# The last feed-forward's down blocks as seven products of halves, with two sums' low parts on GpSimd a block later

## What is computed

```python
def swiglu(h, w_gate, w_up, w_down):
    return (jax.nn.silu(h @ w_gate) * (h @ w_up)) @ w_down

h = modulate(rms_norm(x, g_ffn[l]), sh_f, sc_f)
x = x + gt_f[:, None, :] * swiglu(h, w_gate[l], w_up[l], w_down[l])
```

## The kernel before

| part | gate, up | down |
|---|---|---|
| A, nt 8 | 19 to 26 | 27 to 30 |
| B, nt 8 | 31 to 38 | 39 to 42 |
| C, nt 6 | 43 to 48 | 49 to 52 |

## Time and profile before

### The profile page before, as it was taken

The page is one execution under the profiler, slowest core; times in us unless marked ns, Lnnn a source line. Parts: engine busy times, 40 slices in busy tenths (PEclk is TensorE's granted clock), DMA queues, the critical chain, the costliest instruction groups (busy, mean ns, idle before and its releaser), DMA issues.

```text
span 2032.4 us, 29841 instructions
## 1 busy us (share of the span) xinstructions
PE 2026.5 (100%) x10896; PEld 1712.4 (84%) x10896; DVE 1220.5 (60%) x2142; ACT 894.1 (44%) x1361; POOL 1038.9 (51%) x773
## 2 busy tenths in 40 slices
PE   9999999999999999999999999999999999999999
PEld 7788778889889878877788899898877788989898
DVE  5677335576757637854356767567445478647363
ACT  4124353536446422244445355364446544536352
POOL 5454334476555754443355755556343334656555
PEclk9999999999999999999999999999999999999999
DMA  6332212343543343321233443433221212233233
GB/s 223 107 104 84 83 63 101 117 166 105 187 147 124 104 130 101 104 83 64 82 111 128 142 151 144 166 104 104 97 85 66 80 42 104 84 104 105 104 104 104
DMA packets 37492, 223.99 MB, mean 110 GB/s; under 512 B 6012, under 2 KB 6524, under 8 KB 11744
## 3 DMA queue, kind: packets, MB, share of 16 engines
q1 hardware_dynamic: 31424, 193.48, 27.7%
q10 hardware_dynamic: 5920, 28.55, 4.1%
HBM read 215.59 MB, written 2.10 MB: 107 GB/s over the span
## 4 chain that ended last, share of the span: by engine, by line
PE 98%; DVE 1%; DVEq 0%; issue 0%; ACT 0%; ACTq 0%
PE ps L599 18%; PE ps L601 18%; PE ps L600 18%; PE ps L756 6%; PE ps L758 6%; PE ps L757 6%; PE ps L616 4%; PE ps L617 4%; PE ps L618 4%; PE ps L684 2%; PE ps L648 1%; PE ps L650 1%; PE ps L649 1%; PE ps L705 1%; PE ps L694 1%; PE ps L726 0%
## 5 line engine op out<-in xcount | busy, mean ns | idle before, releaser
L519 POOL TENSOR_TENSOR w_lo<-w_raw,w_hi 128x512 fp32r<-128x512 f32 x544 | 732.0, 1377 | 775.8 <-ACT w_hi L1168 766.5
L1168 ACT ACTIVATE w_hi<-w_raw 128x2048 fp32r<-128x2048 f32 x134 | 256.1, 1911 | 383.5 <-PE ps L601 290.7
L599 PE MATMUL ps<-a_hi,w_hi 128*128 128x512 f32 (+1 forms) x888 | 352.2, 397 | 0.0
L601 PE MATMUL ps<-a_hi,w_lo 128*128 128x512 f32 (+1 forms) x888 | 346.2, 390 | 0.0
L600 PE MATMUL ps<-a_lo,w_hi 128*128 128x512 f32 (+1 forms) x888 | 345.8, 389 | 0.0
L533 POOL TENSOR_TENSOR w_lo<-w_raw,w_hi 128x512 fp32r<-128x512 f32 x164 | 214.6, 1331 | 160.9 <-ACT w_hi L1295 160.9
L599 PE MATMUL ps<-b_hi,w_hi 128*128 128x512 f32 x612 | 238.1, 389 | 0.0
L600 PE MATMUL ps<-b_lo,w_hi 128*128 128x512 f32 x612 | 238.1, 389 | 0.0
L601 PE MATMUL ps<-b_hi,w_lo 128*128 128x512 f32 x612 | 238.1, 389 | 0.0
L599 PEld LDWEIGHTS ps<-a_hi,w_hi 128*128 128x128 f32 (+1 forms) x888 | 165.3, 186 | 48.0 <-issue 9.7
L601 PEld LDWEIGHTS ps<-a_hi,w_lo 128*128 128x128 f32 (+1 forms) x888 | 165.3, 186 | 36.8
(11 more groups left out here) (394 smaller groups left out, 4523.6 us busy)
## 6 DMA issues: line engine op xcount, KB each, us to landing
w_raw<-in_weights SPq DMA_DIRECT2D x176, 1024.0 KB, 4.9
v<-in_ada ACTq DMA_DIRECT2D x24, 1024.0 KB, 4.9
out<-x SPq DMA_DIRECT2D x8, 256.0 KB, 2.5
x<-in_x_in SPq DMA_DIRECT2D x3, 512.0 KB, 6.8
w_raw<-in_weights SPq DMA_DIRECT2D x4, 256.0 KB, 5.5
yc<-in_c_rows ACTq DMA_DIRECT2D x2, 512.0 KB, 3.2
bias<-in_mult_bias ACTq DMA_DIRECT2D x1, 640.0 KB
x<-in_x_in SPq DMA_DIRECT2D x2, 256.0 KB, 4.7
```

Source lines behind the costliest of these rows:

```text
L519: nc.gpsimd.tensor_tensor(w_lo[:, s, piece], w_raw[:, s, piece], f32(w_hi[:, s, piece]), ALU.subtract).then_inc(w_lo_ready, 1)
L599: nc.tensor.matmul(o, wh, hi(kt), start=kt == 0, stop=False)
L601: last = nc.tensor.matmul(o, wl, hi(kt), start=False, stop=kt == depth - 1)
L1168: nc.scalar.activation(w_hi[:, n % 2, :], w_raw[:, n % 2, :], ACT.Copy).then_inc(w_hi_ready, 1)
```

## The change

Eight of the twelve down blocks become fast blocks: 28, 29, 30, 40, 41, 42, 50 and 51. For these, seven products need token sums of h, four for each part. VectorE makes the raw sums (`h_forms`) as the tiles of h come, in every up block's turn. ScalarE rounds three of them ahead of its work on the first fast down block and the fourth, whose place is a quarter of h itself (in part C of `a_hi`), after the first down block. VectorE makes the low parts of the first two, ahead of `sum_low` (2) and of the x adds; GpSimd makes those of the other two ahead of the low parts of the second fast down block. The x add takes the fast block's results from `sums`.

To give the sums room, the scratch for DMA descriptors shrinks from 16 KB to 1 KB per partition, and t4's raw values share a place with other data. h's tiles and the down weights' rows are stored in the order of halves (`h_slot`). The gate block carries its columns twice, 64 apart: the second copy is replaced by its low part in place, so that 16 matmuls of 100 columns give both products, and VectorE adds the two groups of rows.

```diff
-FAST = [j for j, kind, *_ in feed_forward() if kind != "down" and j >= C_FF + 5]
+def fast_kind(j, kind, hid, b, nt):
+    if kind == "down":
+        return 0 < b - nt < (3 if nt == FF_TILES[-1] else 4)
+    return j >= C_FF + 5
+FIRST_DOWNS = [j for j, kind, hid, b, nt in feed_forward() if b == nt]
+FAST = [plan[0] for plan in feed_forward() if fast_kind(*plan)]
...
 GpSimd
+            def split_gates(n, s):
+                pool.wait_ge(w_hi_ready, n - 1)
+                raw, hi = (m[:, s, :].rearrange("p (k c) -> p k c", k=KT)[:, :, LOW_ROW:IF_ROWS] for m in (w_raw, w_hi))
+                nc.gpsimd.tensor_tensor(hi, raw, f32(hi), ALU.subtract).then_inc(w_lo_ready, 4)
+            def h_sum_low(part_, i):
+                hi, lo = (m[:, 0:FF_TILES[part_] // 2, :] for m in h_sums[part_][i])
+                pool.wait_ge(ht_hi, 4 * part_ + T_ORDER.index(i) + 1)
+                nc.gpsimd.tensor_tensor(lo, h_sums_f32[i][:, 0:FF_TILES[part_] // 2, :], f32(hi), ALU.subtract
+                                        ).then_inc(ht_late, 1)
...
+                if n - LAYERS * LAYER_BLOCKS - 2 in FIRST_DOWNS:
+                    for i in T_ORDER[2:4]:
+                        h_sum_low(FIRST_DOWNS.index(n - LAYERS * LAYER_BLOCKS - 2), i)
                 if n in FAST_BLOCKS:
                     split_fast(n, FAST_BLOCKS.index(n))
...
 PE
+            def gate_rows(t, s):
+                pe.wait_ge(bank_free[t % 4], nth(L, LAYER_BANKS, BANK_USES[t]))
+                pe.wait_ge(w_lo_ready, nth(L, 4 * LAYER_BLOCKS, 4 * C_IF + 3))
+                for kt in range(KT):
+                    for part in (a_hi, a_lo):
+                        last = nc.tensor.matmul(ps[t % 4][0:IF_ROWS, :], wcols(w_hi, s, KT, kt, 0, IF_ROWS), part[:, kt, :],
+                                                start=kt == 0 and part is a_hi, stop=kt == KT - 1 and part is a_lo)
+                last.then_inc(tile_done, 2)
...
+                    if j in FAST:
+                        fast_block(L, FF, FAST.index(j), j, FAST_USES[j], (b_hi, b_lo), h_sums[part_], nt // 2,
+                                   lambda i: pe.wait_ge(ht_split if i < 2 else ht_late, 2 * part_ + T_ORDER.index(i) % 2 + 1))
...
 ScalarE, next_weights(j) with f = j + 1
                 column_high(f, 0).then_inc(w_hi_ready, 1)
+                if j in FIRST_DOWNS:
+                    for i in T_ORDER[0:3]:
+                        h_sum_high(FIRST_DOWNS.index(j), i)
                 if j in FAST:
                     p1_copy_out(L, FF, FAST.index(j))
...
+            def h_sum_high(part_, i):
+                act.wait_ge(ht_raw, 4 * part_ + T_ORDER.index(i) + 1)
+                deep = FF_TILES[part_] // 2
+                nc.scalar.activation(h_sums[part_][i][0][:, 0:deep, :], h_sums_f32[i][:, 0:deep, :], ACT.Copy).then_inc(ht_hi, 1)
...
 ScalarE, end of evict(j, u)
+                if j in FIRST_DOWNS and u == 1:
+                    h_sum_high(FIRST_DOWNS.index(j), T_ORDER[3])
...
 VectorE
+                def h_forms(n):
+                    far, i = divmod(n, nt // 2)
+                    t1, t2, t3, t4 = (m[:, i, :] for m in h_sums_f32)
+                    left, right = g[:, 6 + n % 2, 0:HS], g[:, 6 + n % 2, HS:S]
+                    if far == 0:
+                        tt(t1, left, right, ALU.subtract)
+                        nc.vector.tensor_copy(t3, right)
+                        return
+                    nc.vector.scalar_tensor_tensor(t2, right, -1.0, t1, ALU.mult, ALU.subtract)
+                    tt(t3, right, t3, ALU.subtract)
+                    dve.drain()
+                    nc.vector.scalar_tensor_tensor(t4, left, -1.0, t2, ALU.mult, ALU.subtract)
+                def h_sum_low(i):
+                    hi, lo = (m[:, 0:nt // 2, :] for m in h_sums[FIRST_DOWNS.index(j)][i])
+                    dve.wait_ge(ht_hi, 4 * FIRST_DOWNS.index(j) + T_ORDER.index(i) + 1)
+                    tt(lo, h_sums_f32[i][:, 0:nt // 2, :], f32(hi), ALU.subtract).then_inc(ht_split, 1)
...
                 if j + 1 in FAST:
                     sum_low(L, FF, FAST.index(j + 1), 1)
+                if j in FIRST_DOWNS:
+                    h_sum_low(1)
+                    h_sum_low(0)
...
                     for u in range(2):
                         h_low(hid + b - 1 + u)
-                    dve.drain()
+                    for u in range(2):
+                        h_forms(b - 1 + u)
+                    if j + 1 in FIRST_DOWNS:
+                        dve.drain().then_inc(ht_raw, 4)
+                    else:
+                        dve.drain()
                 if kind == "down":
                     for u in range(2):
...
+                        if j in FAST:
+                            nc.vector.scalar_tensor_tensor(x[:, n, :], result[FF][u], (gate, minus_gate[:, n:n + 1])[u],
+                                                           x[:, n, :], ALU.mult, ALU.add)
+                        else:
+                            dve.wait_ge(tile_done, nth(L, LAYER_TILES, t + u))
+                            nc.vector.scalar_tensor_tensor(x[:, n, :], ps[SECOND_BANKS[t + u]][:, :], gate, x[:, n, :],
+                                                           ALU.mult, ALU.add).then_inc(bank_free[SECOND_BANKS[t + u]], 1)
```

More of the change, by code:

```diff
@@ L67, with h_slot @@
 HK, HS = KT // 2, S // 2
+def h_slot(n, nt):
+    return n if n < nt // 2 else HK + n - nt // 2
 T_ORDER = (1, 0, 2, 3)
@@ L203, in two_blocks @@
         ctx.enter_context(one)
+        thirteen = ExitStack()
+        hs = [sb(f"hs{i}", [P, 2, HK, HS], F32R, thirteen) for i in range(2)]
+        thirteen.close()
+        hs_raw = sb("hs_raw", [P, 2, 2, HK * HS])
         four = ExitStack()
@@ L370, in two_blocks @@
         raw_copied = sem("raw_copied")
+        ht_raw = sem("ht_raw")
+        ht_hi = sem("ht_hi")
+        ht_split = sem("ht_split")
+        ht_late = sem("ht_late")
         s_sum = sem("s_sum")
@@ L590, in low_parts, with product @@
                 return low
-            def product(o, s, deep, depth, c0, m, hi, lo, low, tiles=1, between=None, at=5):
-                for kt in range(depth):
+            def product(o, s, deep, depth, c0, m, hi, lo, low, tiles=1, between=None, at=5, slots=None):
+                slots = slots or range(depth)
+                for kt in slots:
                     low(kt, deep)
@@ L598, in product, with tile, tile_pair @@
                     wh, wl = wcols(w_hi, s, deep, kt, c0, m), wcols(w_lo, s, deep, kt, c0, m)
-                    nc.tensor.matmul(o, wh, hi(kt), start=kt == 0, stop=False)
+                    nc.tensor.matmul(o, wh, hi(kt), start=kt == slots[0], stop=False)
                     nc.tensor.matmul(o, wh, lo(kt), start=False, stop=False)
-                    last = nc.tensor.matmul(o, wl, hi(kt), start=False, stop=kt == depth - 1)
+                    last = nc.tensor.matmul(o, wl, hi(kt), start=False, stop=kt == slots[-1])
                 last.then_inc(tile_done, tiles)
-            def tile(L, t, s, deep, c0, hi, lo, low, m=P, depth=None, uses=None, tiles=1, between=None, at=5):
+            def tile(L, t, s, deep, c0, hi, lo, low, m=P, depth=None, uses=None, tiles=1, between=None, at=5, slots=None):
                 pe.wait_ge(bank_free[t % 4], nth(L, LAYER_BANKS, t // 4 if uses is None else uses))
                 product(ps[t % 4][0:m, :], s, deep, depth or deep, c0, m,
[L607 to L612, removed]
+                        lambda kt: hi[:, kt, :], lambda kt: lo[:, kt, :], low, tiles, between, at, slots)
+            def tile_pair(o, s, src, ready, low, depth=KT, deep=None, slots=None):
+                slots = slots or range(depth)
+                for n, kt in enumerate(slots):
+                    ready(n)
                     low(kt, deep or depth)
@@ L754, in part @@
                     (fh, fl), (mh, ml) = form, moving
-                    for kt in range(HK):
+                    for kt in range(depth):
                         nc.tensor.matmul(o, fh[:, kt, :], mh[:, kt, :], start=kt == 0, stop=False)
                         nc.tensor.matmul(o, fh[:, kt, :], ml[:, kt, :], start=False, stop=False)
-                        last = nc.tensor.matmul(o, fl[:, kt, :], mh[:, kt, :], start=False, stop=kt == HK - 1)
+                        last = nc.tensor.matmul(o, fl[:, kt, :], mh[:, kt, :], start=False, stop=kt == depth - 1)
                     return last
@@ L1031, in _ @@
                         if u == 0:
-                            tile(L, t, s, KT, 0, a_hi, a_lo, low, m=F_ROW + MH, tiles=2)
+                            gate_rows(t, s)
                     elif j > 1:
@@ L1125, in _ @@
             j, hid = C_FF, 0
-            for nt in FF_TILES:
+            for part_, nt in enumerate(FF_TILES):
+                slots = [h_slot(n, nt) for n in range(nt)]
                 for b in range(nt):
@@ L1157, in _ @@
                     for u in range(2):
```

(8 more changed lines are left out.)

68 lines of the change are left out of this document (42 added, 26 removed).

## The result

The changed kernel takes 2076.8 us (2076.4 to 2079.0) against 2034.2 in the same comparison: ratio 1.0212, 95% interval 1.0198 to 1.0226. It is slower, as forecast, but by 42.6 us where 25.7 were forecast. Its profiled execution has a span of 2074.6 us, 42.2 more than before.

What follows compares the result with a forecast made beforehand. The prediction took PE as the bound (98% of the last-ending chain). Losses 3.0 + 4.6 + 0.6 + 25.4 = 33.6 us less 7.9 saved gave +25.7, 2059.9 us; range 2047 to 2067, about 0.85.

Steps and rivals of the forecast that it cites:

- block 24: PE's wait for bank 1, freed by a Silu delayed behind forms of blocks 20 and 22: 3.0 us, from 1.7 to 3.5.
- block 26: PE's wait for first_sums, delayed by block 24's far forms on VectorE in part A, which has no room: 4.6 us.
- blocks 36, 38: Far forms after block 36 on VectorE overshoot when PE needs bank 1 of block 38, by up to 0.8: 0.6 us.
- banks, A, B, C: PE waits at blocks 28, 40, 50 for VectorE's late x adds to free bank 0: 8.7, 7.6, 9.1, together 25.4 us.
- saved: Less PE work: 4.9 us in six eight-deep down blocks, 1.2 in two six-deep, 1.8 in the gate block; 7.9 us.
- What would show it: Signs: PE waits of 6 to 10 us at blocks 28, 40, 50, about 5 at 26, 2 to 4 at 24; matmuls 0.12 apart.
- the exclusion: Two-SBUF-input VectorE instructions and SBUF-reading GpSimd ones exclude each other, the later waiting in full; each h_sum_low taken at 1.55 us.
- The surcharge on the two multiplies of the h stage: Part A's h stage runs beside GpSimd's whole split, 2.57 us for 1.50 in part B: 1.1 us more bank wait.
- The reserve that I had set against it: At block 24, ScalarE could have been 0.7 us faster, since its copies waited for PE; set against the delay.
- a reserve of 3.9: Time from first_sums' end at 1879.83 until PE needs bank 1 of block 38 at 1883.71: 3.9 us.
- the fourth rival: VectorE's 6.42 us idle in the first down block hides everything, only savings stand: 2026.3 us; chance 0.03.
- GpSimd's later sums: h_sum_low(2) and (3) on GpSimd, about 2.5 us each, finish before late block 40 wants them: cost nothing.

Runs made afterwards that it cites:

- filler matmuls: Changed kernel with 62, 62 and 84 extra, overwritten 256-column matmuls on PE before the bank 0 waits at blocks 28, 40 and 50; 2073.5 us.
- gates-only kernel: Changed kernel without fast down blocks or sums of h, keeping the 16-matmul gate block, smaller scratch and slot order; 2032.1 us, 2032.0 in a second comparison.
- x adds first: Changed kernel with VectorE's x adds right after the weight sums, ahead of sum_low(1) and both h_sum_low, in first down blocks; 2063.3 us.
- GpSimd held back: Changed kernel with GpSimd making the first weight sum's low part only after VectorE has made both h_sum_low; 2070.5 us.
- part B alone: Changed kernel with fast down blocks 40, 41, 42 and sums of h only in part B, the others as before; 2045.7 us.

## Why the prediction was right in sign and wrong in size

The forecast was +25.7 us and a range up to 2067; it came out at +42.6 between the medians. Term by term, from the trace of after (waits, then the slow steps behind them):

| term | forecast | waits | slow steps |
|---|---|---|---|
| block 24 | 3.0 | 5.2 | 2.2 |
| block 26 | 4.6 | 3.0 | 1.6 |
| blocks 36, 38 | 0.6 | 2.5 | 1.7 |
| banks, A, B, C | 25.4 | 8.4, 8.5, 11.0 | 2.1, 2.1, 1.9 |
| small one in C | 0 | 1.1 | 0.1 |
| saved | 7.9 | 7.9 | |

- **The step that failed is one that I took as given**: under "What would show it" the down blocks' matmuls stand at 0.12 us each, and nowhere is a wait followed by anything. A PE that idles for some us comes back at the lower clock. That is 10.9 of the 16.5 us missing in the spans; the filler matmuls showed the cause. The other 5.6 us are mis-sized waits. By the waits alone the sum would be 39.2 - 7.9 = 31.3, 2065.5 us and inside the range. That is an estimate and on the low side: the 2.2 us behind block 24 delay PE on its way into the wait at block 26, whose end VectorE sets, so without them that wait would have been 5.2 for the 4.6 forecast, and 8.7 of the 10.9 is the most that the lower clock cost in net. The earlier trace rows couldn't show the price, since before PE waited no more than 0.3 us at a time there.
- **Mis-sized, the bank waits**: 27.9 for 25.4. In part B the chain was right to a few tenths up to sum_low(1): raw sums at 8.5 (forecast 8.7), the end of sum_low(1) at 13.6 (14.0). Then each h_sum_low took 2.3 where I had 1.55, chosen between 1.22 and 1.78. GpSimd worked without a break there, so the whole price was due, 1.4 us more in each part. The prediction names the exclusion as a rule, the later one waiting in full, and then priced these two by a row in between; a quad is 1.27, and 1.08 was added to each. Part C has the same two at 2.04 and 2.02 for 1.3 each. The surcharge on the two multiplies of the h stage fell on another part: the 1.1 us forecast for part A (2.57 for 1.50) didn't come, the two took 1.50 there, and in part C, where none was forecast, they took 2.57. So A is below its 8.7 in spite of the 1.4, which is luck, and C is 1.9 above its 9.1.
- **Mis-sized, block 24**: 5.2 for 1.7 to 3.5. The weight sums begin at 1735.86 and in the gates-only kernel's second run, which is as early as after until block 20, at 1730.05: 5.8 later, for a forecast of 2.4 to 4.2. Block 20's near forms account for 2.6 of it, where I had 1.2, since GpSimd works there too, and block 22's for 3.3 (0.42, 0.28, then 1.51 and 1.38 beside GpSimd). The reserve that I had set against it was there, 1.1 for my 0.7.
- **Mis-sized, blocks 36 and 38**: 2.5 for 0.6. Block 36's far forms took 4.5, within my 2.8 to 4.7. But VectorE's turns had slipped against GpSimd's: the multiplies ahead of the forms now ran beside the late quads of block 37 (1889.63 to 1892.7) and took 2.39 in place of 1.50. The weight sums for block 38 began 10.1 us after block 37 and not 4.2, 6.0 later against a reserve of 3.9.
- **Right**: where the waits are and who ends them; that the fourth rival, a reserve that hides the adds, wouldn't hold; contention between VectorE and GpSimd as an exclusion, not a slowdown; the savings of 1.8 us (gates) and 0.82 for each eight-deep block (1.7 for two). And what stands under "GpSimd's later sums", that they wait behind a late PE: they held PE up only in kernels where it was less late or not late at all.

x adds first and GpSimd held back don't reach the kernel before: they give 13.5 and 6.3 us, and if they added up, 2057 us would be left (the two together weren't run). What was needed is cover: one whole block more, which costs 0.82 us and takes away 10 to 13.

## What to carry to other kernels

When a block is changed to need all the banks at once, ask which instruction frees the first one and what now stands ahead of it on its engine; if the banks of the block before are full until its end, leave one block of the old kind between. Price a new wait of the busiest engine twice: the wait, and the work behind it at the lower clock, as far as that work doesn't run into another wait whose end a different engine sets. Count a VectorE instruction with two SBUF operands beside GpSimd as one after the other, and order them so, since running them together gained 0.6 of 6.3 us here; and before a saving is spread to all places where it fits, try it in the one with the most room.

## What the runs showed of the hardware

- After idle times of PE of 2.5 to 11.7 us the granted clock was mostly at its lower level, and 1.4 to 2.4 us were lost behind nearly all of them (0.1 behind 3.6 at block 26 with the x adds first). Around 2 us it went either way: behind the wait of 2.0 us at block 38, 1.6 us of slow steps in the kernel after and in part B alone, 0.1 with the x adds first and with GpSimd held back. What decides between the two these runs don't show. The length of the wait hardly changed the price (2.2 us behind 5.2, 1.9 behind 11.0).
- A VectorE copy of 128x256 with one operand took 0.28 us alone and 1.38 beside GpSimd: here one operand in SBUF was enough. The Trainium skill (SBUF — State Buffer, "Who interferes with whom") says that copies can contend when they run in a two-port mode; whether this one did, no row shows.
- A slow clock ahead of a wait can cost nothing. The wait at block 26 was 2.8 us in after (in brackets, as above) and 3.5 to 3.6 in four of the experiments. VectorE's rows into it agree to 0.01 us between after and the kernel with work for PE, and the wait ends at 1766.3 in both; but behind block 24 after lost 2.2 us in slow steps and the four 1.4 to 1.6, so their PE came to the wait 0.7 us earlier. Slow steps and wait together are 5.2 us in all five.
